# Seven block products for the pooled column chunks, and another place for the cache stores

## The reference

```
h = rmsnorm(x);  proj = h @ w_in              # 1024 columns in, 6672 out
u_pool, u_qkv, b, a, z, gate_pool, gate_delta = split(proj)
y_pool  = (windowed mean of u_pool over 2, 4, 8, 16 tokens - u_pool) @ w_pool * pool_scale
q, k, v = silu(causal_conv(u_qkv));  o, S = gated_delta(q, k, v, ...)      # 8 heads
merged  = sigmoid(gate_pool) * (y_pool @ w_branch_pool) + sigmoid(gate_delta) * (y_delta @ w_branch_delta)
x = x + merged @ w_out;  x = x + experts(rmsnorm(x))                       # 32 experts, 2 per token
returns y, the last 15 pooled rows, the last 3 rows ahead of the convolution, S  (prompt and sample)
```

## Time and profile before

| | |
|---|---|
| median of three runs | 576.93 us |
| span of the profiled execution (first to last instruction) | 575.7 us |
| runs less span: launch and end, outside the span | 1.0 to 2.7 us, 1.2 at the median |
| TensorE busy | 537.8 us, 93% |
| VectorE, ScalarE, GpSimd busy | 276.5, 152.8, 135.6 us |
| DMA | 158.02 MB, mean 274 GB/s, about 420 GB/s in the expert stage |
| granted TensorE clock | 0.982 (1.00 up to 350 us) |

### The profile page before, as it was taken

One profiled execution on the slowest core, in us unless ns is written; L12 is line 12 of the kernel. 1 busy time (PEld: TensorE's weight loads), 2 busy tenths in 40 slices (PEclk: granted clock), 3 DMA queues, 4 the chain that ended last, 5 costly groups with the idle time before them and its releaser, 6 DMA issues. The chain is left out here.

```text
span 575.7 us, 13023 instructions
## 1 busy us (share of the span) xinstructions
PE 537.8 (93%) x5284; PEld 409.5 (71%) x5284; DVE 276.5 (48%) x803; ACT 152.8 (27%) x408; POOL 135.6 (24%) x218
## 2 busy tenths in 40 slices
PE   7999999999999999999999999999999959699974
PEld 6899999877788776779899888656455535265432
DVE  2767668782532626335766244534524231405045
ACT  3258465316851012133200123210111101010105
POOL 6587677013020081033224132000000000000001
PEclk9999999999999999999999999999998989889998
DMA  9735444657984154745387898899999999999992
GB/s 275 220 112 158 129 160 148 211 174 276 313 233 161 12 159 163 221 142 151 109 274 299 350 425 299 344 408 422 397 422 420 421 418 421 422 418 420 405 374 93
DMA packets 81229, 158.02 MB, mean 274 GB/s; under 512 B 11166, under 2 KB 65067, under 8 KB 68979
## 3 DMA queue, kind: packets, MB, share of 16 engines
q1 hardware_dynamic: 78604, 153.69, 72.8%
q10 hardware_dynamic: 2567, 3.51, 2.0%
HBM read 149.40 MB, written 7.96 MB: 273 GB/s over the span
## 5 line engine op out<-in xcount | busy, mean ns | idle before, releaser
L1426 PE MATMUL ps<-arena 128*128 128x288 f32 x480 | 122.6, 410 | 0.9 <-DVE arena L2341 0.7
L1426 PEld LDWEIGHTS ps<-arena 128*128 128x128 f32 x480 | 89.4, 190 | 26.5 <-issue 2.3
L2090 PE MATMUL ps<-arena 128*32 128x256 f32 x1024 | 64.7, 411 | 15.2 <-DMA arena<-in_w_up_dram 13.6
L1433 PE MATMUL ps<-arena 128*128 128x144 f32 x616 | 78.3, 287 | 0.0
L1433 PEld LDWEIGHTS ps<-arena 128*128 128x128 f32 x616 | 76.3, 190 | 2.4 <-issue 1.9
L2090 PEld LDWEIGHTS ps<-arena 128*32 128x32 f32 x1024 | 37.8, 118 | 40.1 <-issue 24.6
L906 POOL TENSOR_TENSOR arena<-arena 128x512 f32<-128x512 f32 x2 | 2.5, 1274 | 207.2 <-ACT arena L1339 207.2
L2366 DVE SCALAR_TENSOR_TENSOR ps<-arena,ps 128x312 f32<-128x312 f32 x72 | 39.1, 544 | 2.2 <-ACT ps L1026 0.9
L1379 PE MATMUL ps<-arena 128*128 128x128 f32 (+7 forms) x162 | 26.7, 284 | 7.4 <-DVE arena L3052 5.1
L2005 PE MATMUL ps<-arena 128*128 128x128 f32 x256 | 32.3, 279 | 0.7 <-DVE arena L3030 0.6
L2005 PEld LDWEIGHTS ps<-arena 128*128 128x128 f32 x256 | 29.8, 192 | 3.6 <-issue 2.5
(11 more groups left out here) (438 smaller groups left out, 807.9 us busy)
## 6 DMA issues: line engine op xcount, KB each, us to landing
arena<-in_w_gate_dram SPq DMA_DIRECT2D x32, 1024.0 KB, 12.9
arena<-in_w_up_dram SPq DMA_DIRECT2D x32, 1024.0 KB, 16.6
arena<-in_w_down_dram SPq DMA_DIRECT2D x28, 1024.0 KB, 17.0
arena<-in_w_in_dram SPq DMA_DIRECT2D x26, 1024.0 KB, 5.7
out_dram<-arena SPq DMA_DIRECT2D x9, 512.0 KB, 7.2
arena<-in_w_branch_delta_dram SPq DMA_DIRECT2D x4, 1024.0 KB, 5.8
arena<-in_w_out_dram SPq DMA_DIRECT2D x4, 1024.0 KB, 5.2
arena<-in_state_delta_dram SPq DMA_DIRECT2D x7, 512.0 KB, 8.5
```

The costliest lines, as they stand in the source:

```text
L1426: last = mm(ps[n % 2][:, 0:T], w[:, k, P * (n % 2):P * (n % 2) + P], hT[:, k, :], start=(k == 0), stop=(k == KD - 1))
L1433: last = mm(to[:, 0:HT], left[:, k, :], right[:, k, :], start=(first and k == 0), stop=(k == HK - 1), skip_group_check=True)
L2090: last = mm(to[CAP * e:CAP * e + CAP, 0:FE], xgT[:, k, CAP * e:CAP * e + CAP], w[e][:, k, :], start=(k == 0), stop=(k == KD - 1))
```

## The change

Items 12 and 13, the pooled groups, are made as fast pairs too. The new fast pairs use ring slots 4 and 5 for their weight sums, as the others do, so items 16 and 17 can be loaded into these slots only after pairs 12 and 13. The buffers of the pooled groups' columns become four (`EP_OF`, the fourth over the convolution's buffers), ScalarE copies only the sample rows (`own_rows`), and VectorE adds the rest. The flip of the heads' rows (`rows_flip`) goes into pair 11, and VectorE's copy of it (`row_ev`) right behind that pair.

On SyncE `head_rows` and then `store_conv` stand behind item 16 (before: `store_conv` and then `head_rows`, behind item 18). `store_pool` stays behind item 19, the states behind items 20 and 21. ScalarE copies the pooled rows for that store behind the first chunk of z and its pooled rows 0 and 1, where it did so ahead of the first chunk of z.

```
-FAST = range(1, NQKV // 2)
+FAST = range(1, (NQKV + NG) // 2)
-SLOT_OF = [i % 4 if i < NQKV // 2 else i % RA for i in range(A_ITEMS)]
+SLOT_OF = [i % 4 if i <= FAST[-1] else i % RA for i in range(A_ITEMS)]
+OWN_ORDER = (0, 1, 3, 2)
-CONV_AT = NQKV // 2 + RA
-ROWS_AT = NQKV // 2 + RA
+CONV_AT = FAST[-1] + 3
+POOL_AT, STATES_AT = CONV_AT + 3, CONV_AT + 4
@@ SyncE
                 if i == CONV_AT:
+                    head_rows()
                     store_conv()
-                if i == CONV_AT + 1:
+                if i == POOL_AT:
                     store_pool()
-                if i == ROWS_AT:
-                    head_rows()
-                if i - CONV_AT in (2, 3):
-                    load_states(i - CONV_AT - 2)
+                if i - STATES_AT in (0, 1):
+                    load_states(i - STATES_AT)
@@ ScalarE
+            def own_rows(g):
+                act.wait_ge(S["sums"], added((NQKV + g) // 2, SUM7 if g % 2 else SUM5))
...
+            own_rows(3)
+            own_rows(2)
             act.wait_ge(S["silu"], 3 * NQKV)
-            for n in range(N_POOL, N_Z):
-                evac(n)
-                if n == N_POOL:
-                    raw_rows(NQKV // 8 - 1)
-            act.wait_ge(S["stage_out"], 16 * 2 * (1 + BD))
-            act.wait_ge(S["newp_t"], NG)
-            nc.scalar.activation(stage[0:PBUF, 0:512], ps[2][0:PBUF, :], ACT.Copy).then_inc(S["newp_ev"], 1)
-            nc.scalar.activation(stage[0:TS, 512:1024], ps[6][0:TS, :], ACT.Copy).then_inc(S["newp_ev"], 1)
+            act.wait_ge(S["sums"], added(FAST[-1], SUM6))
             for n in range(Z_AHEAD):
                 evac(N_Z + n)
                 pool_rows(2 * n)
                 pool_rows(2 * n + 1)
+                if n == 0:
+                    act.wait_ge(S["stage_out"], 16 * 2 * (1 + BD))
+                    act.wait_ge(S["newp_t"], NG)
+                    nc.scalar.activation(stage[0:PBUF, 0:512], ps[2][0:PBUF, :], ACT.Copy).then_inc(S["newp_ev"], 1)
+                    nc.scalar.activation(stage[0:TS, 512:1024], ps[6][0:TS, :], ACT.Copy).then_inc(S["newp_ev"], 1)
@@ TensorE
             for i in FAST:
-                fast_pair(i, {1: scalars, 2: scalars_back, 6: decay_sums, 9: squares_back}.get(i, nothing))
+                fast_pair(i, {1: scalars, 2: scalars_back, 6: decay_sums, 9: squares_back, 11: rows_flip,
+                              13: first_new_pools}.get(i, nothing))
...
-            for g in range(NG):
-                proj(N_POOL + g)
-                if g == 0:
-                    rows_flip()
-                    raw_flip(NQKV // 2 - 1)
-                if g >= 1:
-                    new_pool(g - 1)
-            new_pool(NG - 1)
             for n in range(Z_AHEAD):
                 proj(N_Z + n)
+                if n == 0:
+                    new_pool(3)
+                    new_pool(2)
                 pool_mix(2 * n)
                 pool_mix(2 * n + 1)
@@ VectorE
-            add_u5(FAST[-1])
-            add_u6(FAST[-1])
-            conv(NQKV - 2, 1)
-            conv(NQKV - 1, 1)
...
+                if i == 11:
+                    dve.wait_ge(S["row_pe"], 1)
+                    V.tensor_copy(by_row, ps[7][0:2 * H, 0:TP]).then_inc(S["row_ev"], 1)
+            pair = FAST[-1]
+            add_u5(pair - 1)
+            add_u6(pair - 1)
             link(V.reciprocal(invc, invc))
-            for g in range(NG):
-                window(g)
-                if g == 0:
-                    dve.wait_ge(S["row_pe"], 1)
-                    V.tensor_copy(by_row, ps[5][0:2 * H, 0:TP]).then_inc(S["row_ev"], 1)
-                    sample_scales()
-                if g == 1:
-                    sample_quarters()
+            add_u2(pair)
+            window(0)
+            add_u4(pair)
+            add_u7(pair)
+            window(1)
+            add_u5(pair)
+            add_u6(pair)
+            window(2)
+            window(3)
+            sample_scales()
+            sample_quarters()
```

More of the change, by code:

```diff
@@ L1534, in nothing, with new_pool, pool_mix, rows_flip @@
                 pass
+            def new_pool(g):
+                pe.wait_ge(S["own_ev"], OWN_ORDER.index(g) + 1)
+                if g == 0:
+                    pe.wait_ge(S["raw_ev"], NQKV // 8)
+                    pe.wait_ge(S["silu"], 3 * NQKV)
+                flip(ps[2][0:PBUF, g * P:(g + 1) * P], EP_OF[g][:, TP:TP + PBUF], P)
+                flip(ps[6][0:TS, g * P:(g + 1) * P], C[g % 2][:, 0:TS], P).then_inc(S["newp_t"], 1)
+            def pool_mix(g):
+                pe.wait_ge(S["pool_dve"], g + 1)
+                if g == 0:
+                    pe.wait_ge(S["ss_sc"], 2)
+                    pe.wait_ge(S["misc_in"], 16 * 5)
+                if g == 1:
+                    pe.wait_ge(S["sums"], added(FAST[-1], SUM5))
+                if g >= 2:
+                    pe.wait_ge(S["wp_ev"], g - 1)
+                mm(ps[MIX_BANK[g % 2]][:, 0:T], wpool[:, g, :], pooled[:, g, :], start=True, stop=True).then_inc(S["wp_pe"], 1)
+            def rows_flip():
+                pe.wait_ge(S["by_token"], 1)
+                for c in range(2):
+                    last = flip(ps[7][0:2 * H, P * c:P * c + P], by_token[:, c, :], P)
+                last.then_inc(S["row_pe"], 1)
+            def first_new_pools():
+                new_pool(0)
+                new_pool(1)
             for i in FAST:
-                fast_pair(i, {1: scalars, 2: scalars_back, 6: decay_sums, 9: squares_back}.get(i, nothing))
+                fast_pair(i, {1: scalars, 2: scalars_back, 6: decay_sums, 9: squares_back, 11: rows_flip,
+                              13: first_new_pools}.get(i, nothing))
                 if i == 1:
                     pe.wait_ge(S["ab_ev"], 1)
-                raw_flip(i - 1)
+                if i <= NQKV // 2:
+                    raw_flip(i - 1)
                 if i == 2:
@@ L2373, in later_tokens @@
             def later_tokens(n, src, bank):
[L2375 to L2378, removed]
+                e, at, end = columns_of(n)
+                if n < NQKV:
+                    dve.wait_ge(S["raw_cp"], n - 2)
+                if n == NQKV + 2:
+                    dve.wait_ge(S["newp_t"], 1)
+                if n == NQKV + 3:
+                    dve.wait_ge(S["raw_cp"], NQKV)
+                V.tensor_tensor(e[:, at + HT:end], src[:, 0:TP - HT], bank[:, 0:TP - HT], ALU.add)
+                return V.tensor_tensor(e[:, end:].rearrange("p (b r) -> p b r", b=BD)[:, :, at:],
                                        src[:, TP - HT:HT].rearrange("p (b t) -> p b t", b=BD),
@@ L2501, in sample_quarters, with window, new @@
                         link(V.tensor_copy(to[own, :], src))
-            for i in FAST:
+            def window(g):
+                n = N_POOL + g
+                dve.wait_ge(S["proj_free"], free[n | 1])
+                dve.wait_ge(S["sums"], added(n // 2, SUM6))
+                dve.wait_ge(S["e_cache"], n + 1 if g < 2 else NQKV + NG + 1)
+                e = EP_OF[g]
+                src, w = e, 1
+                for L in range(g + 1):
+                    dst = wa[L % 2]
+                    link(V.tensor_tensor(dst[:, 2 * w - 1:EPW], src[:, 2 * w - 1:EPW], src[:, w - 1:EPW - w], ALU.add))
+                    src, w = dst, 2 * w
+                link(V.tensor_tensor(pooled[:, g, 0:w], src[:, PBUF:PBUF + w], invc[:, 0:w], ALU.mult))
+                link(V.tensor_tensor(pooled[:, g, 0:w], pooled[:, g, 0:w], e[:, PBUF:PBUF + w], ALU.subtract))
+                link(V.scalar_tensor_tensor(pooled[:, g, w:TP], src[:, PBUF + w:PE0], 1.0 / w, e[:, PBUF + w:PE0],
+                                            ALU.mult, ALU.subtract))
+                def new(a):
+                    return a[:, PE0:EPW].rearrange("p (b r) -> p b r", b=BD)[:, :, PBUF:]
+                last_as(V.scalar_tensor_tensor(pooled[:, g, TP:T].rearrange("p (b t) -> p b t", b=BD), new(src), 1.0 / w,
+                                               new(e), ALU.mult, ALU.subtract), "pool_dve", g + 1)
+            for i in FAST[:-1]:
                 if i != FAST[0]:
```

132 lines of the change are left out of this document (54 added, 78 removed).

## The result

| kernel | runs | median us | kernel before, same chip | ratio, 95% interval |
|---|---|---|---|---|
| the change | 6 | 580.49 (578.92 to 582.15) | 577.35 | 1.0050 [1.0034, 1.0065] |
| the change, again | 12 | 579.67 (577.82 to 582.39) | 577.34 | 1.0038 [1.0020, 1.0057] |

The change makes the kernel slower by about 0.4%, 2.3 us in the one set of runs and 3.1 in the other. The forecast was 579.8.

The account below looks back on a forecast made before the run. TensorE has no slack before the expert stage, but SyncE's chain of stores ties it: the late zeroed image starts state products 2.9 us later. 575.7 + 2.9 = 578.6, with 1.2 around the span 579.8 us; range 576.4 to 582.5.

Parts of the forecast that it names:

- TensorE's part: From 107.91 to 125.24 us, 14.51 us of work replaces 17.33, so the first chunk of z starts 2.82 us earlier.
- The added sums of VectorE and GpSimd: Weight sums for pairs 12 and 13 fit into idle time on both engines; costed at nothing.
- SyncE's part: Head rows' store lands with item 16 at 120.6, the 18 stores run 4.8 us later, state products start 2.9 us later.
- The two waits: New TensorE waits: 2.5 us at the first head's products, about 2.6 to 4.8 us at the state products.
- The fall of the clock: TensorE's two new waits bring down the granted clock, costing up to 3 us: 583 us; chance 0.09.
- What lies around the span: Time between the execution's span and the median of the kernel before, 1.2 us, taken to stay.
- No change: Head rows' store lands in its 1.7 us, the first head does not wait, the image decides: 576.5 us; chance 0.20.
- Faster: Zeroed image is not the tie, lands by 155.7, and TensorE keeps its 2.38 us: 574.5 us; chance 0.06.
- Slower still: The new waits at the first head and state products lower TensorE's granted clock, up to 3 us: 583 us; chance 0.09.

Follow-up runs that it names:

- the two moves together: The changed kernel with the head rows' store, wait and loads behind item 15 and the zeroed image's store behind item 17: 573.99 us, again 573.46 us.
- the 156 waits on top of both moves: The changed kernel with head rows behind item 15, image's store behind item 17, and 156 more waits for things long done on TensorE's queue: 574.58 us.

## Why the prediction was right, and what it owes to luck

**TensorE's part held.** 2.82 us at the first chunk of z was forecast, 2.84 stands in the trace. The added sums of VectorE and GpSimd cost nothing, as covered; the two moves together keep the whole saving.

**SyncE's part held in size.** With 0.54 us added to the times of this execution: row loads from 120.4 (forecast 120.6), stores 121.3 to 135.2 (121.4 to 135.3), first head 138.96 (139.1), image 161.6 (161.6), state products 164.07 (163.9). That the small store lands with item 16 was chosen between 117.3 and 122.3, and it landed at 119.89. The reason given, its place in SyncE's queue, was not the cause: on another queue it lands no earlier.

**The two waits held**, 2.38 and 2.83 us. The second alone makes the change slower than before; the first gives back the gain.

**Two terms were missing, and in part they cancel.** The fall of the clock was a rival of 0.09 and in truth a part of the likeliest case: 1.67 us in the profiled run, nothing in those in which it came at the first head. And the kernel before loses 1.2 us for want of instructions at 214 to 222 us, which the change, by its length alone, does not. The profiled execution then reads 3.0 (image) + 1.7 (clock) - 1.2 (fetches) = 3.5, or 2.9 with the 0.54 of its early start; its span is 3.2 us longer. I had seen the 0.61 us there and passed over it. The idle of the kernel before could have gone to the other side with any edit that changes the number of TensorE's instructions.

In the second trace of the change the state products start 2.2 us late (163.26 against 161.04), or 3.1 with the 0.9 by which this execution is early from its first pair on. Less the 1.2 of the fetches it is 1.0 us late, and so it stands from 222 to 420 us. Its span is yet 2.3 us longer. The other 1.3 us come in the expert stage, where the traces drift by -0.7 to +1.3 us against that of the kernel before, whatever the edit; the cause stays open. So the 2.9 us of the forecast stand where they were forecast, at the state products (3.0 and 3.1 us); that the medians differ by nearly the same, 3.1 and 2.3 us, is in part luck.

**What lies around the span** is 1.7 to 1.8 us in the runs of the kernel before made beside the experiments, and 1.7 to 2.1 in the change's; I took 1.2, by setting one execution's span against another's time. The forecast span of 578.6 stands against 578.9 and 578.0 in the two traces of the change.

**The rivals.** No change (576.5): the store did not land in 1.7 us behind a load, on either queue. Faster (574.5): the image was the tie; with both moves, it and the head rows untied, it is 573.5 to 574.0. Slower still (583): the clock did fall, in both traces of the change, but it cost at most 1.7 us.

## What to carry to other kernels

An engine that gets faster gives nothing until the next thing it waits for is early too: read for each later rendezvous how much slack it has, and move what ties it (here a 256 KB store, which could stand some 18 us earlier) together with the change. A small store that its issuer must wait for belongs where that engine would stand still anyway, since behind a megabyte it lands with the megabyte. And before a difference of 1 us is put down to an edit, see whether TensorE's idle moments marked as issue follow a fetch of instructions: an edit that only changes the count of instructions moves these.

## What the runs showed of the hardware that was not expected

- A 16 KB store lands 1.7 us after its issue in an empty queue (five traces), and 4.2 to 6.4 us after it where a 1 MB load was issued 0.4 to 1.1 us ahead, always within about 0.2 us of that load's own landing, on the same queue or another.
- TensorE's instructions come in fetches of 16 KB, 42 in a run (43 with the 156 waits on top of both moves). The Trainium skill, Runtime: NRT & Kernel Launch, section Instruction fetch mechanics, gives 256 instructions a fetch, and the traces agree (10825 instructions of TensorE in the kernel before, 258 a fetch). The Trainium skill also has the fetch hidden behind dispatch; here it is not, where 128 small products with their weight loads, 256 instructions, run in 1.29 us: up to 1.6 us of idle. Why one fetch comes so late in the one case stays open.
- The granted clock fell to 1.2 GHz at waits of 2.49, 2.58 and 2.83 us, for 3.4 us that began 1.1 to 1.9 us behind the wait's end, and at waits of 5.18 and 6.53 us, for 6.8 us that began 0.8 and 1.7 us before it. It did not fall at waits of 1.64, 2.38 and 2.45.
